# Moving the score output of the RWKV mixer from its own visit into the fourth level of the triangular inverse

## Chip, cores and metric

One core of a Trainium2 chip runs the whole kernel. The metric is the device time of one execution in microseconds (us), and its median over several executions.

## The reference

A trunk of two layers works on 256 tokens of width 2048. Layer 0 projects the tokens and mixes them in two ways: 8 heads of stick-breaking attention (head width 128) and 16 heads of an RWKV-7 recurrence (head width 64). Layer 1 is a gated delta rule. Behind each mixer follow an output projection, a layer norm, and a squared-ReLU MLP with a second layer norm. Only layer 0's mixer is touched here:

```python
z = jnp.einsum('bhqd,bhsd->bhqs', q_blk, kf) * (d ** -0.5)
log_keep = jnp.where(mask, jax.nn.log_sigmoid(-z), 0.0)
log_a = z + lax.cumsum(log_keep, axis=3, reverse=True)
a = jnp.exp(jnp.where(mask, log_a, -jnp.inf))
return jnp.einsum('bhqs,bhsd->bhqd', a, vf)
...
h = jnp.concatenate([o_sb, o_rw], axis=-1).astype(x.dtype) @ ev_w_out[e]
```

The last einsum of the attention, `a` by `vf`, is the "score output" of this document. Its result is needed only by the output projection `ev_w_out`.

## The kernel before

**Projections.** All large products split their f32 weights into a high part `wh` and a low part `wl` (both f32r) and add three products. Weights come in panels of 8 units from HBM into `raw`; for each unit ScalarE writes the high part (L888), VectorE subtracts it to give the low part (L1358), and TensorE then runs the matmuls of the unit (L422). A unit may start on TensorE only when VectorE has signalled its low part (`lo_ready`). Both engines make the split of unit u + 2 while TensorE works on unit u.

**The mixer inside the projections.** Layer 0 is cut into 8 groups of heads. While TensorE projects group i (16 units, 32 half units of 9 matmuls), it also runs the mixer `mix0` of group m = i - 1: one attention head and two RWKV heads. So there are 8 mixer bodies, m = 0 to 7. The first six are a hardware loop, the seventh stands behind it, and m = 7 runs inside the output projection, whose matmuls are wider. On every engine `mix0` is a generator, cut by `yield` into 28 visits, numbered 0 to 27 here. The tuple `HOPS0` says how many half units TensorE runs behind each visit:

```python
HOPS0 = (3, 3, 2, 2, 2) + 16 * (1,) + (0, 1, 0, 1, 0, 1, 1)
```

So unit 4 lies behind visit 3, unit 5 behind visit 4, half of unit 6 behind visit 5. ScalarE and VectorE run their own pieces of a visit and behind them the splits that belong to it: the split of unit 5 is behind visit 2, of unit 6 behind visit 3, of unit 7 behind visit 4. The order on each engine is fixed by this program text; engines meet only at semaphores.

**The visits that matter.** Visit 1: TensorE makes the scores (up to L508), VectorE takes them at L1511. Visit 2: VectorE's operand chain, up to `loga` (L1536) and `operands` (L1540), fed by ScalarE's exponentials. Visit 3: ScalarE's exponential L981 gives the attention weights `sba` and signals `attn`. Visit 4: TensorE waits for `attn` and runs L522 (two query blocks by the values `vtk` of block 0) and L523 (the second block), both f32, into PSUM bank `mb[3]`; they are called the pair. ScalarE copies the result to `hTh` (L984, `sb_hi`), and VectorE subtracts for `hTl` (L1544, `sb_lo`). Visit 5: TensorE waits for `operands` and `sb_lo` and makes the chunk matrices (L535, L540), the latter into `mb[3]`. Visit 6: transposes of the tokens; those of k and b go into bank `mb[1]` and stay there until ScalarE has copied them to `BK` (L1001, L1003, L1005, in levels 2 to 4). Visits 7 to 17 are the inverse of a triangular matrix, in levels: visit 6 + 2 lv has L582 (`dX`), visit 7 + 2 lv the transposes of X (L558) and the next L566 (`AX`). So level 4 is visits 14 and 15 on TensorE. VectorE answers with L1566 (`Yn`) and L1573 (`X_ready`), ScalarE with the transposed copy L1008. Between them VectorE runs pieces of the next group's token shift (`next(pieces, None)`). Visit 18 uses the inverse (L593), and writes banks 0 and 1. Visits 19 to 25 are the four chunks of the recurrence (L623 to L640), visits 26 and 27 the norm of the output (L645, L646, L649).

Of the kernel before, what the change touches and what calls it, by code (L numbers as in the profile page):

```python
# [16 lines left out]
ALU = mybir.AluOpType  # L17
ACT = mybir.ActivationFunctionType

P = 128  # L20
D = 2048
T = 256
# [142 lines left out]
def trunk(nc, stop, x, w384, w512, wba, consts, c0, c1, prm0, lora, conv, rows1, normw, ln, out):  # L165
    ctx = ExitStack()
    with ctx:
        def sb(name, shape, dt=F32):
            return ctx.enter_context(nc.sbuf_tensor(name, shape, dt))
# [3 lines left out]
        def S(name):  # L173
            if name not in sems:
                sems[name] = ctx.enter_context(nc.semaphore(name))
            return sems[name]
# [7 lines left out]
        hTh = sb("hTh", [P, KT, T], F32R)  # L184
        hTl = sb("hTl", [P, KT, T], F32R)
# [5 lines left out]
        mb = [mpf[:, b * WIDE:(b + 1) * WIDE] for b in range(4)]  # L191
# [7 lines left out]
        def half(i):  # L199
            return slice(HC * i, HC * i + HC)  # L200
# [5 lines left out]
        def r2(ap, **kw):  # L206
            return ap.rearrange("p (a b) -> p a b", **kw)
# [34 lines left out]
        BK, UV = (r2(lay(4 * P), a=4) for _ in range(2))  # L242
# [11 lines left out]
        vtk = r2(lay(T), a=TT)  # L254
        sba, sbb, sbc = (lay(384) for _ in range(3))
# [121 lines left out]
        def _(pe):  # L377
            mm = nc.tensor.matmul

            def to_tiles():  # L380

                pe.sem_inc(S("tiles"), 1)
# [109 lines left out]
            def mix0(m):  # L492
                m1 = m + 1
# [9 lines left out]
                   skip_group_check=True).then_inc(S("lora_used"), 1)  # L503
# [5 lines left out]
                   skip_group_check=True).then_inc(S("scores"), 1)  # L509
# [8 lines left out]
                mm(mb[2][:, 0:384], tri, sbb, start=True, stop=False, skip_group_check=True)  # L518
                mm(mb[2][:, P:T], ones, sbb[:, T:384], start=False, stop=True, skip_group_check=True).then_inc(S("lcum"), 1)
                yield  # L520
                pe.wait_ge(S("attn"), m1)
                mm(mb[3][:, 0:T], vtk[:, 0, :], sba[:, 0:T], start=True, stop=False, skip_group_check=True)  # L522
                mm(mb[3][:, P:T], vtk[:, 1, :], sba[:, T:384], start=False, stop=True,  # L523
                   skip_group_check=True).then_inc(S("sb_o"), 1)
                yield
                pe.wait_ge(S("operands"), m1)
                pe.wait_ge(S("sb_lo"), m1)
                to_tiles()
                turned = lambda n: slice((n + 3) % 4 * HC, (n + 3) % 4 * HC + HC)
                for t in range(TT):  # L530
                    for w in range(2):
                        for h, hf in QUADS:
# [3 lines left out]
                                      start=t + w == 0, stop=True, skip_group_check=True)  # L536
# [19 lines left out]
                def transpose_x():  # L556
                    for h in range(2):
                        last = nc.tensor.transpose(mb[0][:, h * P:(h + 1) * P],  # L558
                                                   X0[:, 2 * h:2 * h + 2, :].rearrange("p t c -> p (t c)"), ident)
                    last.then_inc(S("Xnew"), 1)  # L560

                def a_times_x(lv):
                    for h in range(2):
                        for e, t in QUADS:
                            Xp = X0[half(e), 2 * h + t, :].rearrange("p (b w s) -> p b w s", w=2, s=1 << lv)
                            last = mm(mb[2 + e][half(t), h * T:h * T + 32], GM[half(e), 2 * t + 1 - e, h, 0, :], Xp[:, :, 0, :],  # L566
                                      start=h == 0, stop=True, skip_group_check=True)
                    last.then_inc(S("AX"), 1)
# [7 lines left out]
                for lv in range(1, 6):  # L576
                    pe.wait_ge(S("Yn"), 5 * m + lv)
                    pe.wait_ge(S("XT_ready"), 6 * m + lv)
                    to_tiles()
                    for h in range(2):  # L580
                        for t, e in QUADS:
                            last = mm(mb[2 + t][half(e), h * T:h * T + 32], XT0[half(t), h, e, :], Yn0[half(t), 2 * e + h, :],  # L582
                                      start=h == 0, stop=True, skip_group_check=True)
                    last.then_inc(S("dX"), 1)
                    yield
                    pe.wait_ge(S("X_ready"), 6 * m + lv + 1)
                    transpose_x()
                    if lv < 5:
                        a_times_x(lv + 1)
                    else:  # L590
                        for h in range(2):
                            for hf, t in QUADS:
                                last = mm(mb[2 + hf][half(t), h * T:h * T + HC], GM[half(hf), 2 * t + hf, h, 0, :],  # L593
                                          UV[half(hf), 2 * t + hf, half(h)], start=h == 0, stop=True, skip_group_check=True)
                        last.then_inc(S("AV"), 1)
                    yield
# [1 line left out]

                pe.wait_ge(S("XT_ready"), 6 * m1)
                pe.wait_ge(S("AVs"), m1)  # L600
                pe.wait_ge(S("tok_ready"), 2 * m1)
                to_tiles()
                for h in range(2):
                    for t, hf in QUADS:
                        last = mm(mb[2 + t][half(1 - hf), h * T:h * T + HC], XT0[half(t), h, 1 - hf, :],
                                  AVs[half(t), (2 * hf + h) * HC:(2 * hf + h + 1) * HC], start=h == 0, stop=True,
                                  skip_group_check=True)
                last.then_inc(S("XAV"), 1)
                for hf in range(2):
                    for t, h in QUADS:  # L610
                        last = mm(mb[t][half(h), half(hf)], tokw[half(t), hf, half(h)], XT0[half(t), h, 1 - hf, :],
                                  start=hf == 0, stop=True, skip_group_check=True)
# [3 lines left out]
                for n in range(4):  # L616
                    t, hf = divmod(n, 2)
                    st_in, y_ = (Sb, Sa)[n % 2], mb[2][:, n * P:(n + 1) * P]
                    if n:
                        pe.wait_ge(S("state0"), 3 * m + n)  # L620
                        if n < 3:

                            last = mm(mb[0][:, 0:P], KR[:, hf, 0, :, :].rearrange("p t c -> p (t c)"), st_in, start=True, stop=True,  # L623
                                      skip_group_check=True)
                        else:
                            last = mm(mb[0][half(1 - hf), 0:P], KR[:, hf, 0, t, :], st_in, start=True, stop=True,
                                      skip_group_check=True)
# [6 lines left out]
                    if n < 3:  # L634
                        mm(mb[3][:, 0:P], BK[:, n, :], UV[:, n, :], start=True, stop=True,
                           skip_group_check=True).then_inc(S("dS"), 1)
                    if n:
# [3 lines left out]
                       skip_group_check=True).then_inc(S("y_psum"), 1)  # L641
# [16 lines left out]
            with pe.Fori(1, GROUPS - 1) as i:  # L658
                drive(group0(i), 2 * UNITS, 0, mix0(i - 1), HOPS0)
            drive(group0(GROUPS - 1), 2 * UNITS, 0, mix0(GROUPS - 2), HOPS0)  # L660

            pe.wait_ge(S("mix0_out"), GROUPS - 2)
# [216 lines left out]
        def _(act):  # L879
            go = nc.scalar.activation  # L880
            st = Steps(act, S("act_steps"))
# [64 lines left out]
            def mix0(m):  # L946
                m1 = m + 1
# [32 lines left out]
                act.wait_ge(S("loga"), m1)  # L980
                go(sba, sba, ACT.Exp).then_inc(S("attn"), 1)  # L981
                yield
                act.wait_ge(S("sb_o"), m1)
                nc.scalar.copy(hTh[:, bass.ds(m * 2, 1), :], mb[3][:, 0:T].unsqueeze(1)).then_inc(S("sb_hi"), 1)  # L984
                yield
                yield

# [9 lines left out]
                nc.scalar.copy(XTf0, mb[0][:, 0:T]).then_inc(S("XT_ready"), 1)  # L997
                yield
                for lv in range(1, 6):
                    if lv == 2:  # L1000
                        st(nc.scalar.copy(BK[half(0), :, :], r2(mb[1][half(0), :], a=4)))  # L1001
                    elif lv == 3:
                        st(nc.scalar.copy(BK[half(1), 1:4, :], r2(mb[1][half(1), 0:3 * P], a=3)))  # L1003
                    elif lv == 4:
                        nc.scalar.copy(BK[half(1), 0, :], mb[1][half(1), 3 * P:4 * P]).then_inc(S("tok_ready"), 1)  # L1005
                    yield
                    act.wait_ge(S("Xnew"), 6 * m + lv + 1)
                    nc.scalar.copy(XTf0, mb[0][:, 0:T]).then_inc(S("XT_ready"), 1)  # L1008
                    if lv == 5:
                        act.wait_ge(S("AV"), m1)  # L1010
                        nc.scalar.copy(r2(AVs, a=4), r2(mp[1][:, :], a=4)[:, :, 0:HC]).then_inc(S("AVs"), 1)
                    yield
# [311 lines left out]
            def solo():  # L1324
# [3 lines left out]
                for _ in range(7):  # L1328
# [6 lines left out]
                       True, begun=True)  # L1335
# [8 lines left out]
        def _(dve):  # L1344
            tt, ts, stt = nc.vector.tensor_tensor, nc.vector.tensor_scalar, nc.vector.scalar_tensor_tensor
            st = Steps(dve, S("dve_steps"))

            def f(ap):
                return ap.bitcast(F32)

            def rep(ap, n):

                return ap.unsqueeze(1).to_broadcast([P, n, ap.shape[-1]])
# [151 lines left out]
            def mix0(m, ahead=True):  # L1505
                m1 = m + 1
                par = lambda j: prm[:, bass.ds(m, 1), j]
                pieces = shift(m1) if ahead else iter(())
# [24 lines left out]
                for w, a, b_ in ((1, rkv[:, 0, :], pinc), (0, kkt, pexc)):  # L1533
# [6 lines left out]
                tt(btr[:, 3 * HC:T], bt[:, 0:HC], pinv[:, 0:HC], ALU.mult).then_inc(S("operands"), 1)  # L1540
                yield
                yield
                dve.wait_ge(S("sb_hi"), m1)
                tt(hTl[:, bass.ds(m * 2, 1), :], mb[3][:, 0:T].unsqueeze(1), f(hTh[:, bass.ds(m * 2, 1), :]),  # L1544
                   ALU.subtract).then_inc(S("sb_lo"), 1)
                yield
                dve.wait_ge(S("gram"), m1)
                for h in range(2):
# [14 lines left out]
                for lv in range(1, 6):  # L1563
                    s_ = 1 << lv
                    dve.wait_ge(S("AX"), 5 * m + lv)
                    tt(Yn0, r2(mp[1][:, :], a=4)[:, :, 0:32], rep(cc[:, C_LV + 32 * (lv - 1):C_LV + 32 * lv], 4),  # L1566
                       ALU.mult).then_inc(S("Yn"), 1)
                    if lv > 2:
                        next(pieces, None)
                    yield  # L1570
                    dve.wait_ge(S("dX"), 5 * m + lv)
                    left = X0.rearrange("p (h t) (b w s) -> p h t b w s", h=2, w=2, s=s_)[:, :, :, :, 0, :]
                    tt(left, left, mp[1][:, :].rearrange("p (t h c) -> p h t c", t=TT, h=2)[:, :, :, 0:32].rearrange("p h t (b s) -> p h t b s", s=s_),  # L1573
                       ALU.add).then_inc(S("X_ready"), 1)
                    if lv > 2:
                        next(pieces, None)
                    yield
                next(pieces, None)
                yield
                dve.wait_ge(S("XAV"), m1)  # L1580
# [500 lines left out]
```

## Time and profile before

| | |
|---|---|
| median of 3 runs | 3047.07 us (3045.55 to 3051.02) |
| the profiled execution's own time | 3048.84 us |
| its span, first to last instruction | 3047.10 us |
| TensorE busy | 2957.6 us, 97% |
| VectorE busy | 1797.7 us, 59% |
| ScalarE busy | 1453.1 us, 48% |
| mean granted TensorE clock | 0.992 |

The times of three runs differ by up to 5.5 us, 0.2%. A busy share says how full an engine is, not who holds up whom; for that the table of waits, the timeline of one body and the chain that ended last are read, in the rows below. Windows and start times are in us from the span's start; the body shown is m = 2, near 191 to 256 us, unless another is named.

### The profile page before, as it was taken

How to read it: one execution, taken by the hardware profiler on the slowest of the kernel's cores; microseconds unless marked ns; L12 is line 12 of the kernel's file. 1: busy time of each engine (PE TensorE's matmuls, PEld its weight loads, DVE VectorE, ACT ScalarE, POOL GpSimd, SP SyncE). 2: the span in 40 equal slices, each digit the busy share in tenths (PEclk: the TensorE clock that was granted, in tenths of full speed). 3: DMA queues.
4: the chain of work that ended last, by engine and by line, in shares of the span. 5: the costliest groups of instructions: out<-in, count | busy, mean ns of one | idle time of the engine just before them, and what ended most of it. 6: DMA issues, size and time to landing. Idle time of an engine off the chain costs nothing.

```text
span 3047.1 us, 55921 instructions
## 1 busy us (share of the span) xinstructions
PE 2957.6 (97%) x22084; PEld 2603.3 (85%) x22084; DVE 1797.7 (59%) x2375; ACT 1453.1 (48%) x2241; POOL 13.1 (0%) x28
## 2 busy tenths in 40 slices
PE   7999999999999999999999999999999999999997
PEld 7888887788888888889999997999977888888886
DVE  4555565565554555564667665566667545555555
ACT  4544454344443444435566664456653434444342
POOL 0000000000000000000000000000000000000000
PEclk9999999999999999999999999999999999999999
DMA  6333334455555555543343433544335555555553
GB/s 214 109 116 111 103 112 144 175 191 189 192 188 191 189 193 191 190 162 136 121 139 132 139 134 136 178 142 137 127 125 219 189 193 187 193 187 191 189 187 111
DMA packets 156999, 491.86 MB, mean 161 GB/s; under 512 B 15584, under 2 KB 50528, under 8 KB 155776
## 3 DMA queue, kind: packets, MB, share of 16 engines
q1 hardware_dynamic: 154032, 476.18, 46.0%
q0 software_dynamic: 2224, 11.69, 1.0%
q8 instruction: 160, 2.62, 0.3%
q10 hardware_dynamic: 544, 1.05, 0.1%
q14 instruction: 39, 0.32, 0.0%
HBM read 486.76 MB, written 2.10 MB: 160 GB/s over the span
## 4 chain that ended last, share of the span: by engine, by line
PE 91%; DVE 5%; ACT 2%; issue 1%; DMA 0%; ACTq 0%; SPq 0%; DVEq 0%
PE pp L422 45%; PE mp L422 11%; PE pp L406 8%; PE mp L406 8%; PE pp L408 4%; PE mp L408 4%; PE mp L821 1%; PE mp L785 1%; PE mp L769 1%; PE mp L761 1%; DVE wl L1358 1%; ACT wh L888 1%; PE mp L827 1%; PE mp L582 0%; PE mp L566 0%
## 5 line engine op out<-in xcount | busy, mean ns | idle before, releaser
L1358 DVE TENSOR_TENSOR wl<-raw,wh 128x1024 fp32r<-128x1024 f32 (+1 forms) x936 | 1101.3, 1184 | 843.0 <-ACT wh L888 839.8
L888 ACT CAST wh<-raw 128x1024 fp32r<-128x1024 f32 (+1 forms) x936 | 943.9, 1018 | 856.3 <-PE pp L422 283.4
L422 PE MATMUL pp<-aT,wh 128*128 128x256 f32 x4704 | 898.1, 291 | 11.4 <-DVE wl L1358 6.7
L422 PEld LDWEIGHTS pp<-aT,wh 128*128 128x128 f32 x4704 | 733.4, 192 | 27.7 <-issue 7.4
L422 PE MATMUL pp<-aT,wl 128*128 128x256 f32 x2352 | 665.7, 283 | 0.0
L422 PEld LDWEIGHTS pp<-aT,wl 128*128 128x128 f32 x2352 | 450.3, 191 | 0.0
L406 PE MATMUL pp<-aT,wh 128*128 128x512 f32 x1024 | 364.8, 400 | 0.6 <-issue 0.4
L422 PE MATMUL pp<-wh,hTh 128*128 128x512 f32 x896 | 358.5, 400 | 4.0 <-DVE wl L1358 2.6
L406 PE MATMUL mp<-aT,wh 128*128 128x512 f32 x1024 | 360.0, 396 | 0.0
L422 PE MATMUL pp<-wh,hTl 128*128 128x512 f32 x896 | 349.6, 390 | 0.0
L422 PE MATMUL pp<-wl,hTh 128*128 128x512 f32 x896 | 349.1, 390 | 0.0
L408 PE MATMUL pp<-aT,wl 128*128 128x256 f32 x1024 | 288.3, 282 | 0.0
L408 PE MATMUL mp<-aT,wl 128*128 128x256 f32 x1024 | 286.5, 280 | 0.0
L406 PEld LDWEIGHTS pp<-aT,wh 128*128 128x128 f32 x1024 | 194.3, 190 | 48.6 <-issue 2.0
L406 PEld LDWEIGHTS mp<-aT,wh 128*128 128x128 f32 x1024 | 192.2, 188 | 46.5
L422 PEld LDWEIGHTS pp<-wh,hTh 128*128 128x128 f32 x896 | 168.2, 188 | 42.1 <-DVE wl L1358 2.9
L422 PE MATMUL mp<-wh,hTh 128*128 128x512 f32 x512 | 199.2, 389 | 0.0
L422 PE MATMUL mp<-wl,hTh 128*128 128x512 f32 x512 | 199.2, 389 | 0.0
L422 PE MATMUL mp<-wh,hTl 128*128 128x512 f32 x512 | 199.2, 389 | 0.0
L422 PEld LDWEIGHTS pp<-wh,hTl 128*128 128x128 f32 x896 | 168.2, 188 | 35.9
L422 PEld LDWEIGHTS pp<-wl,hTh 128*128 128x128 f32 x896 | 168.4, 188 | 32.9 <-issue 0.5
L408 PEld LDWEIGHTS pp<-aT,wl 128*128 128x128 f32 x1024 | 195.1, 190 | 0.1
(301 smaller groups left out, 2671.9 us busy)
## 6 DMA issues: line engine op xcount, KB each, us to landing
raw<-in_w_dram SPq DMA_DIRECT2D x800, 512.0 KB, 3.3
raw<-in_w_dram SPq DMA_DIRECT2D x136, 384.0 KB, 3.5
ws<-in_ln_dram POOLq DMA_DIRECT2D x8, 1024.0 KB, 7.6
out_dram<-xres SPq DMA_DIRECT2D x8, 256.0 KB, 2.0
ws<-in_lora_dram POOLq DMA_DIRECT2D x8, 192.0 KB, 3.5
xres<-in_x_dram ACTq DMA_DIRECT2D x2, 512.0 KB, 6.2
xres<-in_x_dram SPq DMA_DIRECT2D x2, 512.0 KB, 7.1
ws<-in_c_dram POOLq DMA_DIRECT2D x1, 576.0 KB, 6.9
```

The costliest lines, as they stand in the source:

```text
L406: mm(o, wh[:, slot, kk, c], aT[:, k, :, :].rearrange("p a b -> p (a b)"), start=first is not None and kk == 0, stop=False, skip_group_chec ...
L408: last = mm(o[:, 0:T], wl[:, slot, kk, c], ah[:, k, :], start=False, stop=end and kk == 1, skip_group_check=True)
L422: last = mm(o, lhs, rhs, start=opens and m == 0, stop=end and kk == 1 and m == 2, skip_group_check=True)
L761: last = nc.tensor.transpose(mb[2][:, h * P:(h + 1) * P], Xc[:, 2 * h:2 * h + 2, :].rearrange("p c t -> p (c t)"), ident)
L769: last = mm(mb[hf][half(c), h * P:h * P + 32], At[half(hf), c, h, half(hf)], Xp[:, :, 0, :], start=h == 0, stop=True, skip_group_check=True)
L785: last = mm(mb[2 + c][half(hf), h * P:h * P + 32], XTc[half(c), h, hf, :], Yn1[half(c), 4 * hf + h, :], start=h == 0, stop=True, skip_grou ...
L821: last = mm(bank[:, h * P:(h + 1) * P], lhs[:, h, :], rhs[:, h, :], start=h == 0, stop=True, skip_group_check=True)
L827: last = mm(bank[:, j * T:(j + 1) * T], lhs[:, j, :], rhs[:, 2 * j:2 * j + 2, :], start=j == 0, stop=True, skip_group_check=True)
L888: nc.scalar.copy(wh[:, q % RING, :, 0:width], raw[:, q, :, 0:width]).then_inc(S("hi_ready"), 1)
L1358: tt(wl[:, q % RING, :, 0:width], raw[:, q, :, 0:width], f(wh[:, q % RING, :, 0:width]), ALU.subtract).then_inc(S("lo_ready"), 1)
```

## The change

The pair leaves visit 4 and goes into level 4 of the inverse, visit 14, behind L582. It writes bank `mb[1]` instead of `mb[3]`, so the k and b copies to `BK` move one level up, and the pair waits for `tok_ready` as well as for `attn`. ScalarE's copy to `hTh` moves to visit 15, behind the transposed copy; VectorE's subtraction for `hTl` moves to visit 15 too, behind `Yn` of level 5, where it takes the place of one piece of the token shift, which is made up for in visit 17. TensorE's wait for `sb_lo` moves from visit 5 to visit 18. Visit 4 stays, with its two half units and no mixer work on TensorE, ScalarE or VectorE.

```diff
@@ TensorE, visit 4 and 5
                 yield
-                pe.wait_ge(S("attn"), m1)
-                mm(mb[3][:, 0:T], vtk[:, 0, :], sba[:, 0:T], start=True, stop=False, skip_group_check=True)
-                mm(mb[3][:, P:T], vtk[:, 1, :], sba[:, T:384], start=False, stop=True,
-                   skip_group_check=True).then_inc(S("sb_o"), 1)
                 yield
                 pe.wait_ge(S("operands"), m1)
-                pe.wait_ge(S("sb_lo"), m1)
                 to_tiles()
@@ TensorE, level lv, behind L582
                     last.then_inc(S("dX"), 1)
+                    if lv == 4:
+                        pe.wait_ge(S("attn"), m1)
+                        pe.wait_ge(S("tok_ready"), 2 * m1)
+                        mm(mb[1][:, 0:T], vtk[:, 0, :], sba[:, 0:T], start=True, stop=False, skip_group_check=True)
+                        mm(mb[1][:, P:T], vtk[:, 1, :], sba[:, T:384], start=False, stop=True,
+                           skip_group_check=True).then_inc(S("sb_o"), 1)
                     yield
@@ TensorE, visit 18
                 pe.wait_ge(S("AVs"), m1)
-                pe.wait_ge(S("tok_ready"), 2 * m1)
+                pe.wait_ge(S("sb_lo"), m1)
@@ ScalarE, visit 4
                 yield
-                act.wait_ge(S("sb_o"), m1)
-                nc.scalar.copy(hTh[:, bass.ds(m * 2, 1), :], mb[3][:, 0:T].unsqueeze(1)).then_inc(S("sb_hi"), 1)
                 yield
@@ ScalarE, levels
                 for lv in range(1, 6):
-                    if lv == 2:
+                    if lv == 1:
                         st(nc.scalar.copy(BK[half(0), :, :], r2(mb[1][half(0), :], a=4)))
+                    elif lv == 2:
+                        st(nc.scalar.copy(BK[half(1), 1:4, :], r2(mb[1][half(1), 0:3 * P], a=3)))
                     elif lv == 3:
-                        st(nc.scalar.copy(BK[half(1), 1:4, :], r2(mb[1][half(1), 0:3 * P], a=3)))
-                    elif lv == 4:
                         nc.scalar.copy(BK[half(1), 0, :], mb[1][half(1), 3 * P:4 * P]).then_inc(S("tok_ready"), 1)
                     yield
                     act.wait_ge(S("Xnew"), 6 * m + lv + 1)
                     nc.scalar.copy(XTf0, mb[0][:, 0:T]).then_inc(S("XT_ready"), 1)
-                    if lv == 5:
+                    if lv == 4:
+                        act.wait_ge(S("sb_o"), m1)
+                        nc.scalar.copy(hTh[:, bass.ds(m * 2, 1), :], mb[1][:, 0:T].unsqueeze(1)).then_inc(S("sb_hi"), 1)
+                    elif lv == 5:
@@ VectorE, visit 4
                 yield
-                dve.wait_ge(S("sb_hi"), m1)
-                tt(hTl[:, bass.ds(m * 2, 1), :], mb[3][:, 0:T].unsqueeze(1), f(hTh[:, bass.ds(m * 2, 1), :]),
-                   ALU.subtract).then_inc(S("sb_lo"), 1)
                 yield
@@ VectorE, levels, behind Yn
-                    if lv > 2:
+                    if lv == 5:
+                        dve.wait_ge(S("sb_hi"), m1)
+                        tt(hTl[:, bass.ds(m * 2, 1), :], mb[1][:, 0:T].unsqueeze(1), f(hTh[:, bass.ds(m * 2, 1), :]),
+                           ALU.subtract).then_inc(S("sb_lo"), 1)
+                    elif lv > 2:
                         next(pieces, None)
                     yield
@@ VectorE, visit 17
                     yield
+                next(pieces, None)
                 next(pieces, None)
                 yield
```

## Rows read from the trace of the kernel before

**Rows 1.** The page: shares of the chain that ended last.

```profile
PE 91%; DVE 5%; ACT 2%; issue 1%; DMA 0%; ACTq 0%; SPq 0%; DVEq 0%
```

**Rows 2.** TensorE's waits, 59 to 506 us: waiting line, releaser, total us, times, longest.

```profile
PE mp L522 <- ACT ws L981: 8.2, 7, 1.2
PE mp L645 <- ACT ws L1027: 6.0, 7, 0.9
...
PE pp L422 <- DVE wl L1358: 2.2, 8, 0.5
```

**Rows 3.** TensorE's timeline, visit 4: start, us, instruction, [idle before <- releaser].

```profile
208.71 0.28 PE L422 MATMUL pp<-aT,wl 128*128 128x256 f32 x1
210.15 0.70 PE L522 MATMUL mp<-ws 128*128 128x256 f32 x2 [1.17 <-ACT ws L981]
210.69 0.39 PE L523 MATMUL mp<-ws 128*128 128x128 f32 x2
211.33 0.51 PE L422 MATMUL pp<-aT,wh 128*128 128x256 f32 x2 [0.25 <-DVE wl L1358]
```

**Rows 4.** VectorE's timeline at the same time (x2: two splits in a row).

```profile
210.19 0.22 DVE L1540 TENSOR_TENSOR ws<-ws 128x64 f32<-128x64 f32 x1
210.32 1.82 DVE L1358 TENSOR_TENSOR wl<-raw,wh 128x768 fp32r<-128x768 f32 x2
```

**Rows 5.** The chain that ended last, in order of time: start, us, what.

```profile
200.20 0.57 DVE ws L1511
...
210.41 0.88 DVE wl L1358
211.33 2.42 PE pp L422 x18
...
252.47 4.30 PE pp L422 x36
...
259.72 0.57 DVE ws L1511
```

**Rows 6.** TensorE's timeline in the last body, m = 7, around the pair.

```profile
517.50 0.47 PE L422 MATMUL pp<-wh,hTh 128*128 128x512 f32 x1 [1.36 <-DVE wl L1358]
...
520.12 0.39 PE L422 MATMUL pp<-wh,hTl 128*128 128x512 f32 x1
520.35 0.59 PE L522 MATMUL mp<-ws 128*128 128x256 f32 x2
...
520.92 0.48 PE L422 MATMUL pp<-wh,hTh 128*128 128x512 f32 x1
521.24 0.39 PE L422 MATMUL pp<-wl,hTh 128*128 128x512 f32 x1
```

**Rows 7.** TensorE's timeline at visit 14 of m = 2.

```profile
230.55 0.43 PE L582 MATMUL mp<-ws 64*64 64x32 f32 x16
```

**Rows 8.** Timelines of ScalarE, VectorE and TensorE at visits 12 to 17.

```profile
226.67 0.48 ACT L1003 COPY ws<-mp 64x384 f32<-64x384 f32 x1
232.51 0.37 ACT L1008 COPY ws<-mp 128x256 f32<-128x256 f32 x1 [2.09 <-PE mp L558]
232.78 0.84 ACT L888 CAST wh<-raw 128x768 fp32r<-128x768 f32 x1
234.54 0.29 DVE L1573 TENSOR_TENSOR ws<-ws,mp 128x128 f32<-128x128 f32 x1
235.58 0.38 PE L558 MATMUL mp<-cc,ws 128*128 128x128 f32 x2
```

**Rows 9.** Two gaps of TensorE, and the stretches behind (window, length, busy, granted clock).

```profile
12.72 0.77 PE L422 MATMUL pp<-aT,wh 128*128 128x256 f32 x2 [2.99 <-DVE wl L1358]
12.70:18.00 5.30, 5.28 (x26) 5.30 (x27) 2.84 (x3) 1.67 (x2) 0.00 (x0) 1.00 1.05 389
1333.80 1.11 PE L472 MATMUL mp<-cc,xres 128*128 128x128 f32 x4 [4.71 <-DVE xres L1442]
1333.80:1342.00 8.20, 6.59 (x28) 5.40 (x29) 8.06 (x12) 3.86 (x6) 0.00 (x0) 0.51 0.00 0
```

## The prediction

> **What bounds the kernel now.** I read four views, in this order. First the page: TensorE holds 91% of the chain that ended last [rows 1]. So the question for any edit is whether it takes work or waiting off TensorE, or puts some onto it, at a place where nothing else is later. Second, the table of waits of TensorE over the stretch of the first seven RWKV bodies (m = 0 to 6) [rows 2]. The largest entry is the very wait that the change removes: L522, the score output, stands 8.2 us in 7 waits behind the exponential of L981, 1.17 us each. Read alone, that promises 8.2 us. Third, therefore, the timeline of TensorE around one of these waits, at m = 2 [rows 3]. TensorE ends unit 4 at 208.71 + 0.28 = 208.99, waits, starts the pair L522 and L523 at 210.15, and starts the projection's unit 5 at 211.33, with a second wait of 0.25 us just before it, released by VectorE's split L1358. Fourth, what VectorE does at that time [rows 4]: it comes out of the operand chain with L1540 at 210.19 and only then, at 210.32, starts the low halves of the weights of units 5 and 6. The chain that ended last goes just there [rows 5]: VectorE's L1540, L1358 until 210.41 + 0.88 = 211.29, then TensorE's L422 from 211.33. It does not pass through L981, L522 or L523. One body lasts 59.52 us, from VectorE's L1511 at 200.20 to the next one at 259.72 [rows 5]. The pair and the wait ahead of it lie in a gap that ends with the split of unit 5, whatever TensorE does in it. This is the reading on which the forecast rests: two waits in a row, of which the second, small one is the one that counts.
>
> **Is that gap the same in every body?** The seven waits on L522 sum to 8.2 us with the longest 1.2, and the waits of L422 on L1358 in the same stretch come right behind them [rows 2]. The largest other wait in the body, L645 on the copy L1027, is a round trip that starts from a matmul of TensorE itself. The eighth body (m = 7) differs: its wait for the split, 1.36 us, is before unit 5's counterpart at 517.50, and L522 follows at 520.35 with no wait, inside back-to-back matmuls [rows 6].
>
> **The change part by part.**
>
> 1. *Visit 4 loses the wait on attn and the two matmuls.* In m = 0 to 6 TensorE reaches unit 5 at 208.99 instead of 211.1, and waits there for VectorE's split, which ends at 211.29 because L1540 ends at 210.41, and L1540 and the split stand in VectorE's row with no idle time ahead of them, so that nothing out of visit 4 holds them [rows 4, 5]. Start of unit 5: 211.33 before, 211.33 after. Gain 0. The idle time becomes 211.33 - 208.99 = 2.34 us in one piece. In m = 7 the pair stands in a dense stream. The price of the pair in a dense stream is read there: L422 matmuls follow each other every 0.23 us, as from 520.12 to the start of the pair at 520.35. From 520.12 to 521.24 there lie two such steps (0.46) and the pair: 1.12 - 0.46 = 0.66 us [rows 6]. Gain there 0.66 us.
>
> 2. *Visit 14 gains the two matmuls.* In the stretch of visits 5 to 18 no wait of TensorE stands among the groups of [rows 2] nor in its timeline, and the place of insertion, right behind L582 at 230.55, is in the middle of it [rows 7]. So each body pays the price of the pair in a dense stream: 0.66 us, eight times 5.3 us. Bounds: not below 0; not above the 0.93 us from the start of L522 at 210.15 to the end of L523 at 211.08 [rows 3], that is if nothing of the pair overlaps its neighbours. I take 0.66, as it is the same pair measured in a dense stream. The step from quadrant matmuls to full ones comes at visit 14 anyway (L582 to L422), so none is added.
>
> 3. *The new waits at visit 14.* attn is given before the pair at 210.15 [rows 3], 20 us ahead of visit 14. The k and b copies move one level up; the last one, L1005 (64x128), goes where L1003 (64x384) ran before, from 226.67 to 227.15 [rows 8]; the pair would start at about 230.9. Nothing waits: cost 0, cover 3.7 us. Should that cover go, ScalarE's last copy would be late for TensorE by its own length, under 0.48. The bank is next written at visit 18.
>
> 4. *The copy to hTh on ScalarE and the subtraction to hTl on VectorE move to visit 15.* At visit 4 they were off the chain: gone, they give nothing, since unit 7's split is behind them, not unit 5's. At visit 15 ScalarE copies X transposed at 232.51, then the new copy, then its split L888, which started at 232.78 [rows 8]. A 128x256 copy takes 0.37 but the next one starts after 0.27, so the split comes 0.27 later, and VectorE's split behind it too. Behind that is L1573, the update of X, at 234.54 + 0.29 = 234.83, which then ends near 235.10; TensorE wants it at 235.58 for L558 [rows 8]. Slack 0.75, of which 0.27 are used. The transposed copy that TensorE needs at visit 16 is ahead of the new one in ScalarE's order. VectorE's subtraction of 128x256 takes the place of a token-shift piece of the same size, and that piece goes to visits 16 and 17, behind the update of X. Cost 0; if the cover were gone, see rival A. No DMA and no queue is touched.
>
> 5. *The wait on sb_lo goes from visit 5 to 18.* It was met in time: the table of waits has no entry for L535 [rows 2]. Gain 0, and 0 at visit 18, two visits after the subtraction.
>
> **Does the delay survive to the next body?** The chain answers: TensorE's 36 projection matmuls from 252.47, the group up to L508, and at 259.72 VectorE's L1511, from where ScalarE and VectorE go in turn to L1540 [rows 5]. All of it starts from TensorE, so unit 5 of the next body comes as much later as visit 14 was longer.
>
> **The sum.** Added 8 x 0.66 = 5.28, saved 1 x 0.66 (m = 7): +4.6 us. The profiled execution took 3048.84 for a span of 3047.10, 1.74 us around it that the change does not touch; it would become 3053.4. It lies 1.8 us above the median of the runs, 3047.07, so the forecast for the median is 3047.07 + 4.6 = **3051.7 us**, +0.15%. With the pair at its upper bound in the seven bodies and at visit 14 of the eighth: 8 x 0.93 - 0.66 = 6.8, 3053.9; at the lower bound -0.66, 3046.4.
>
> **A rule that speaks against a longer gap.** TensorE's granted clock was 0.51, so the lower level of 1.2 GHz, from 1333.80 on, after 4.71 us without work; it was 1.00 (2.4 GHz) in the stretch behind the 2.99 us ahead of 12.72 [rows 9]. The 2.34 us of the new gap is below both, so I keep the full clock. The Trainium skill says, in "TensorE: Matmul & The Clock Gate", section "What's actually happening", that the clock is gated to half rate when the engine has been idle, and that activity releases it. By that rule the lengthened gap is a risk that the old one, broken up by the pair, was not; the trace agrees for the long gaps and shows no fall at the shorter one. It stands below as a rival.
>
> **The rivals.**
>
> *A. The handoffs at visits 15 to 17 reach TensorE (slower).* The new copy must be done before VectorE can subtract, and both stand ahead of the splits. In series the copy and a subtraction of the same size are 2 x 0.37 = 0.74 against a slack of 0.75 at L558 [rows 8]; with a handoff or two of 0.1 to 0.2 and the split pushed as well, TensorE would lose up to 0.4 a body. It decides from 0.75 on. Time: 3051.7 + 8 x 0.4 = 3054.9. Against it: the subtraction only replaces a piece of the same size. Chance 0.15.
>
> *B. The clock falls in the new gap (slower).* The low stretch behind L472 lasted at least 8.20 us [rows 9]; at half rate it costs half of that, 4.1 us, seven times 28.7: 3080. Chance 0.02.
>
> *C. The pair costs nothing at visit 14, or its delay is taken up by the wait at L645 (no change).* That is 0.86 us a body [rows 2], more than 0.66. Against it: L1027 copies what TensorE wrote just before, so it moves with TensorE. Time 3047. Chance 0.14.
>
> *D. The gap was TensorE's own after all (faster).* If the split of unit 5 ended earlier once visit 4 is empty, the 1.17 us come back, and with a split done by 208.99 the whole gap, less the pair: 7 x (2.34 - 0.66) = 11.8, 3035; with only the waits on L981 gained, and the pair neutral, 3047.07 - 8.2 = 3038.9. The point from which it decides: the split must end 0.66 us earlier, by 210.6. For it speaks that the profile names L981 as the releaser; against it, that VectorE comes to the split from the operand chain without an idle moment [rows 4], and that chain reads nothing from visit 4. Chance 0.07.
>
> **How the numbers follow.** Forecast 0.62, A 0.15, B 0.02, C 0.14, D 0.07. About 0.2% (6.1 us) is what a measurement of this kernel can tell from no change; the three runs before spread over 5.5 us. The forecast's 4.6 us is under it, but its upper bound 6.8 is over it: 0.08 of its 0.62 falls on slower, the rest on same. Slower 0.08 + 0.15 + 0.02 = 0.25. Of D 0.05 lies beyond 0.2%. Faster 0.05, same 0.70. The range takes in C below with the spread of a median (3046.0) and A above (3055.5); B, D and A's far end are left out. The forecast's own range is 3050 to 3054.
>
> **What the profile after would show.** Right: the wait of L522 on L981 is gone and in its place each of seven bodies has one wait of L422 on L1358 of about 2.3 us; the period of a body is 59.52 + 0.66 = 60.2 us; L582 at level four is followed by the pair with no wait; L558 at visit 17 has none; the first matmul of unit 5 starts as long after L1511 as before (211.33 - 200.20 = 11.13 us [rows 5]). Wrong: the L422 wait is much below 2.3 us (D), a wait at L558 or L593 behind VectorE or ScalarE (A), a granted clock under 1.00 in the bodies (B), a period that stays at 59.5 (C).

## The result and the profile after

The changed kernel takes 3061.1 us in the median of 6 runs (3059.59 to 3062.28), against 3047.06 us before: ratio 1.0043, 95% interval 1.0033 to 1.0053, slower by 14.0 us. The forecast was 3051.7 with a range up to 3055.5. Its direction was right, a third of its size was found, and the rest came from the rival that had been given a chance of 0.02.

TensorE's waits in the changed kernel, 59 to 520 us (waiting line, releaser, total, times, longest):

```profile
PE pp L422 <- DVE wl L1360: 16.8, 8, 2.3
PE mp L646 <- ACT ws L1029: 6.0, 7, 0.9
```

The 8.2 us behind the exponential are gone, and the waits for the split have grown from 2.2 to 16.8 us [rows 2]. So far this is what the prediction said of visit 4. TensorE's timeline there, m = 2:

```profile
213.46 0.28 PE L422 MATMUL pp<-aT,wl 128*128 128x256 f32 x1
216.07 0.51 PE L422 MATMUL pp<-aT,wh 128*128 128x256 f32 x2 [2.33 <-DVE wl L1360]
216.41 0.29 PE L422 MATMUL pp<-aT,wl 128*128 128x256 f32 x1
216.54 0.57 PE L422 MATMUL pp<-aT,wh 128*128 128x256 f32 x2
216.91 0.42 PE L422 MATMUL pp<-aT,wl 128*128 128x256 f32 x1
217.12 0.63 PE L422 MATMUL pp<-aT,wh 128*128 128x256 f32 x2
217.55 0.41 PE L422 MATMUL pp<-aT,wl 128*128 128x256 f32 x1
...
219.47 0.41 PE L422 MATMUL pp<-aT,wl 128*128 128x256 f32 x1
219.81 0.41 PE L530 MATMUL mp<-ws 64*64 64x128 f32 x4
```

The gap is 2.33 us, as forecast. But half a microsecond behind it the same matmuls take 0.41 instead of 0.28 us, and follow each other at nearly twice the distance. From the start of unit 5 to the start of the chunk matrices in L530 it takes 219.81 - 216.07 = 3.74 us; in the kernel before it took 2.35 (211.33 to 213.68, where that line is L535). The windows show why (window, length, then busy time and count by engine; the granted clock is the third number from the end):

```profile
214.00:216.00 2.00, 0.00 (x0) 0.00 (x0) 1.97 (x6) 1.68 (x3) 0.00 (x0) 1.00 0.00 0
216.00:217.00 1.00, 0.93 (x6) 0.93 (x7) 1.00 (x3) 1.00 (x2) 0.00 (x0) 0.80 0.00 0
217.00:219.70 2.70, 2.70 (x14) 2.59 (x13) 0.76 (x1) 0.04 (x1) 0.00 (x0) 0.50 0.75 220
```

TensorE did nothing from 213.7 to 216.07, and from 216.6 to some 220 the granted clock was 0.50, the lower level of 1.2 GHz. A stretch at 0.50 lies at unit 5 in all seven bodies with the gap. It does not always begin at the same point: in m = 0 the clock was still 1.00 for 1.0 us behind the start of unit 5, and in m = 5 it was already at 0.50 0.2 us ahead of it, with TensorE still idle. The Trainium skill says, in "TensorE: Matmul & The Clock Gate", section "What's actually happening", that an idle engine is gated to half rate; here the trace agrees, behind idle stretches of 2.33 us.

VectorE's side of the same moment, and the chain:

```profile
214.93 0.22 DVE L1542 TENSOR_TENSOR ws<-ws 128x64 f32<-128x64 f32 x1
215.06 2.69 DVE L1360 TENSOR_TENSOR wl<-raw,wh 128x768 fp32r<-128x768 f32 x3
```

```profile
204.95 0.57 DVE ws L1513
...
215.15 0.88 DVE wl L1360
216.07 3.81 PE pp L422 x18
...
236.83 0.36 PE mp L577 x16
237.20 0.63 PE mp L583 x2
237.83 0.22 PE mp L584 x2
238.05 1.07 PE pp L422 x9
```

Beside [rows 4, 5]: the operand chain hands over to the split and the split to unit 5 exactly as before (216.07 - 204.95 = 11.12 us from L1513, against 11.13), the 18 matmuls of unit 5 last 3.81 instead of 2.42 us, and the pair, now L583 and L584, lies on the chain at visit 14. Visits 12 to 17, answering to [rows 8]:

```profile
232.88 0.26 ACT L1004 COPY ws<-mp 64x128 f32<-64x128 f32 x1
239.38 0.37 ACT L1007 COPY ws<-mp 128x256 f32<-128x256 f32 x1 [3.03 <-PE mp L553]
239.91 0.85 ACT L889 CAST wh<-raw 128x768 fp32r<-128x768 f32 x1
241.67 0.28 DVE L1576 TENSOR_TENSOR ws<-ws,mp 128x128 f32<-128x128 f32 x1
242.44 0.38 PE L553 MATMUL mp<-cc,ws 128*128 128x128 f32 x2
```

The update of X ends at 241.95 and TensorE uses it at 242.44 without a wait: 0.49 of slack is left, where 0.48 was forecast.

The bodies m = 0 to 5 last 61.58 to 61.70 us instead of 59.52, and from m = 6 to m = 7 it is 66.30 instead of 64.32. The wait for the split in m = 7 ends at 532.87 instead of 517.50, 15.4 us later. Behind the mixer the changed kernel's profiled execution is 2.3 us shorter (0.6 of it in the first MLP, 1.7 in the last part of the span), in code that the change does not touch; so the whole span is only 3060.2 - 3047.1 = 13.1 us longer.

### The profile page after: what moved, and what is told of

Read it like the earlier page. It is cut to its first block, busy times and chain, and to the rows that moved or that the text cites. A ratio compares the mean times of both kernels' runs of the same rounds, so it can differ in the third digit from the quotient of the medians.

```text
span 3060.2 us, 55929 instructions
## 1 busy us (share of the span) xinstructions
PE 2964.5 (97%) x22084; PEld 2612.9 (85%) x22084; DVE 1798.9 (59%) x2375; ACT 1452.0 (47%) x2241; POOL 13.1 (0%) x28
## 4 chain that ended last, share of the span: by engine, by line
PE 91%; DVE 5%; ACT 2%; issue 1%; DMA 0%; ACTq 0%; SPq 0%; DVEq 0%
PE pp L422 45%; PE mp L422 11%; PE pp L406 8%; PE mp L406 8%; PE pp L408 4%; PE mp L408 4%; PE mp L822 1%; PE mp L786 1%; PE mp L770 1%; PE mp L762 1%; DVE wl L1360 1%; ACT wh L889 1%; PE mp L828 1%; PE mp L577 0%; PE mp L561 0%
## 5 line engine op out<-in xcount | busy, mean ns | idle before, releaser
L422 PE MATMUL pp<-aT,wh 128*128 128x256 f32 x4704 | 907.2, 293 | 26.1 <-DVE wl L1360 21.4
L422 PEld LDWEIGHTS pp<-aT,wh 128*128 128x128 f32 x4704 | 741.1, 194 | 42.2 <-DVE wl L1360 20.1
L422 PE MATMUL pp<-aT,wl 128*128 128x256 f32 x2352 | 670.4, 285 | 0.0
L422 PEld LDWEIGHTS pp<-aT,wl 128*128 128x128 f32 x2352 | 454.9, 193 | 0.0
L422 PE MATMUL pp<-wh,hTh 128*128 128x512 f32 x896 | 358.4, 400 | 4.0 <-DVE wl L1360 2.6
L422 PE MATMUL pp<-wh,hTl 128*128 128x512 f32 x896 | 349.6, 390 | 0.0
L422 PE MATMUL pp<-wl,hTh 128*128 128x512 f32 x896 | 349.2, 390 | 0.0
L422 PEld LDWEIGHTS pp<-wh,hTh 128*128 128x128 f32 x896 | 168.2, 188 | 42.1 <-DVE wl L1360 2.9
L422 PE MATMUL mp<-wh,hTh 128*128 128x512 f32 x512 | 199.2, 389 | 0.0
L422 PE MATMUL mp<-wl,hTh 128*128 128x512 f32 x512 | 199.2, 389 | 0.0
L422 PE MATMUL mp<-wh,hTl 128*128 128x512 f32 x512 | 199.2, 389 | 0.0
L422 PEld LDWEIGHTS pp<-wh,hTl 128*128 128x128 f32 x896 | 168.2, 188 | 36.0
L422 PEld LDWEIGHTS pp<-wl,hTh 128*128 128x128 f32 x896 | 168.4, 188 | 32.9 <-issue 0.5
```

The costliest lines, as they stand in the source:

```text
L422: last = mm(o, lhs, rhs, start=opens and m == 0, stop=end and kk == 1 and m == 2, skip_group_check=True)
```

## The experiments

Theory 1: of the 2.15 us that a body got longer, 0.66 are the pair on the chain, and 1.5 the half clock behind the lengthened gap. Theory 2: they come from the pair's place at visit 14, and the clock is a bystander. The body time, from one L1511 to the next in m = 0 to 5, is taken from the trace of each kernel (an edit shifts line numbers: the same line is L1513 in the changed kernel, L1507 in no_pair). Bodies of one kind agree to 0.2 us within an execution, so this is the sharper measure; the runs of one kernel spread over 3 to 9 us. Low clock is counted in m = 0 to 6. A median in brackets is that of the kernel before in the same series of runs.

| kernel | gap before unit 5 | bodies at low clock | body, us | median, us (before) | ratio, 95% |
|---|---|---|---|---|---|
| before | 1.17 + 0.25 | 0 of 7 | 59.52 | 3047.06 | |
| changed | 2.33 | 7 of 7 | 61.58 to 61.70 | 3061.1 | 1.0043 (1.0033 to 1.0053) |
| no_pair | 2.34 | 6 of 7 | 60.87 to 61.04, one 59.51 | 3061.76 (3046.94) | 1.0043 (1.0030 to 1.0057) |
| fill_pair | 1.68 | 0 of 7 | 60.16 | 3054.51 (3046.94) | 1.0025 (1.0015 to 1.0035) |
| pair_twice | 1.17 + 0.25 | 0 of 7 | 60.17 | 3053.39 (3046.94) | 1.0020 (1.0011 to 1.0029) |
| fill_tiny | 1.15 + 0.77, a small matmul between | 6 of 7 | 61.65, one 60.17 | 3058.52, one run | |
| fill_small | 2.11 | 5 of 7 | 61.65, two 60.18 | 3059.58, one run | |
| after_early | 1.00 | 0 of 7 | 58.87 | 3043.78 (3048.05) | 0.9985 (0.9976 to 0.9994) |
| before_early | 1.17 | 0 of 7 | 58.99 | 3045.5 (3048.05) | 0.9994 (0.9985 to 1.0003) |

**no_pair: only the gap.**

```diff
@@ the kernel before, TensorE, visit 4
-                pe.wait_ge(S("attn"), m1)
-                mm(mb[3][:, 0:T], vtk[:, 0, :], sba[:, 0:T], start=True, stop=False, skip_group_check=True)
-                mm(mb[3][:, P:T], vtk[:, 1, :], sba[:, T:384], start=False, stop=True,
-                   skip_group_check=True).then_inc(S("sb_o"), 1)
@@ ScalarE, visit 4
-                act.wait_ge(S("sb_o"), m1)
+                act.wait_ge(S("scores"), m1)
```

> The kernel before with the pair (L522, L523) and its wait on attn left out of visit 4 and put nowhere; the copy to hTh takes what the scores left in the bank, so the score output is not computed. Theory 1 (the longer gap lowers the clock, and that costs 1.5 us in each of seven bodies; the pair itself costs 0.66 us where it is on the chain): TensorE idles 2.3 us before unit 5 in m = 0 to 6, granted clock 0.5 behind it, body 59.5 + 1.5 = 61.0 us, total +10.5 - 0.66 (m = 7) = +9.8 us, about 3057. Theory 2 (the 2.15 us a body of the changed kernel come from the pair's new place at visit 14, by a switch of tile mode or by the handoffs behind it, and the clock is a bystander): body 59.5 us, total -0.7 us, about 3046.

Work was taken away and the kernel got slower. Two bodies of one execution tell it best. Behind a gap of 2.34 us each, m = 2 and m = 5:

```profile
214.19 0.51 PE L422 MATMUL pp<-aT,wh 128*128 128x256 f32 x2 [2.34 <-DVE wl L1354]
...
215.12 0.63 PE L422 MATMUL pp<-aT,wh 128*128 128x256 f32 x2
215.55 0.41 PE L422 MATMUL pp<-aT,wl 128*128 128x256 f32 x1
...
397.24 0.50 PE L422 MATMUL pp<-aT,wh 128*128 128x256 f32 x2 [2.34 <-DVE wl L1354]
397.58 0.28 PE L422 MATMUL pp<-aT,wl 128*128 128x256 f32 x1
...
398.41 0.40 PE L422 MATMUL pp<-aT,wh 128*128 128x256 f32 x2
398.65 0.28 PE L422 MATMUL pp<-aT,wl 128*128 128x256 f32 x1
```

```profile
397.00:401.00 4.00, 3.76 (x67) 3.56 (x68) 2.49 (x5) 1.47 (x3) 0.00 (x0) 1.00 0.49 162
214.00:218.00 4.00, 3.81 (x22) 3.58 (x26) 2.21 (x4) 1.42 (x2) 0.00 (x0) 0.61 0.51 156
```

Where the clock fell the body lasts 61.0 us; in m = 5, where it did not, 59.51, the time of before to 0.01. So the gap without the clock costs nothing, and the clock costs 1.5 us. Theory 2 falls: with nothing at visit 14 the slow bodies are still there. In the mixer this makes 8.8 us (526.34 against 517.50). The median is 14.8 us up, 5 more than expected. In the profiled execution 8 us are in the first MLP (729.4 us from transpose to transpose, against 721.2). TensorE's waits there, 630 to 1340 us:

```profile
PE pp L408 <- issue: 3.0, 2, 1.6
PE pp L406 <- issue: 1.0, 2, 0.5
```

These four waits end with nothing that the profile shows; the kernel before has one, of 0.4 us. Behind the last two of them the granted clock was 0.50 once more, from 1167.2 to 1170.6. Together that is some 5 of the 8 us. What causes such waits in code that the edit doesn't touch, and whether the other runs had them, is open, so no more than the 8.8 us in the mixer is laid to the gap.

**pair_twice: only the pair at visit 14.**

```diff
@@ the kernel before, TensorE, behind L582
                     last.then_inc(S("dX"), 1)
+                    if lv == 4:
+                        pe.wait_ge(S("tok_ready"), 2 * m1)
+                        mm(mb[1][:, 0:T], vtk[:, 0, :], sba[:, 0:T], start=True, stop=False, skip_group_check=True)
+                        mm(mb[1][:, P:T], vtk[:, 1, :], sba[:, T:384], start=False, stop=True, skip_group_check=True)
```

> The kernel before with a second copy of the pair at visit 14, into the bank of the k and b tokens, with the wait on tok_ready; its result is not used. The gap at visit 4 is as before. Theory 1: the granted clock stays at 1.00 in the bodies, each of the 8 bodies pays the pair once more at 0.66 us: body 60.2 us, total +5.3 us, about 3052.3. Theory 2: the place at visit 14 costs 2.15 us: body 61.7 us, total +17 us, about 3064.

The body is 60.17 us, 0.65 longer, with the clock at full rate in all seven bodies. The price of 0.66 us for the pair in a dense stream, read in the body m = 7, holds at visit 14. The median is 6.5 us up, 5.3 expected, inside its interval (3.4 to 8.8).

**fill_pair: the changed kernel, gap filled in part.**

```diff
@@ the changed kernel, TensorE, visit 4
+                mm(mb[3][:, 0:T], vtk[:, 0, :], sbb[:, 0:T], start=True, stop=False, skip_group_check=True)
+                mm(mb[3][:, P:T], vtk[:, 1, :], sbb[:, T:384], start=False, stop=True, skip_group_check=True)
                 yield
```

> The changed kernel with a pair of idle matmuls of the same two shapes put at the start of visit 4, without a wait, into the bank that nobody reads from (values by the finished log-keep terms). Theory 1: the gap before unit 5 is cut to 2.33 - 0.64 = 1.7 us, the granted clock stays at 1.00, body 59.52 + 0.66 = 60.2 us; m = 7 pays the filler, 0.66: total +4.6 + 0.7 = +5.3 us over the kernel before, about 3052.3. If 1.7 us is still long enough for the clock to fall: about 3063. Theory 2: body stays 61.7 us, total +14.7 us, about 3061.8.

```profile
209.95 0.39 PE L522 MATMUL mp<-ws 128*128 128x128 f32 x2
212.02 0.51 PE L422 MATMUL pp<-aT,wh 128*128 128x256 f32 x2 [1.68 <-DVE wl L1362]
```

Useless work of 0.64 us in the gap makes each body 1.5 us shorter than in the changed kernel. It costs nothing there, and the clock stays. The median is 7.6 us up on the kernel before (4.6 to 10.7), where 5.3 was expected.

**fill_tiny and fill_small: how much is enough?**

```diff
@@ fill_tiny: the changed kernel, TensorE, visit 4
+                pe.wait_ge(S("attn"), m1)
+                mm(mb[3][:, 0:32], vtk[:, 0, :], sbb[:, 0:32], start=True, stop=True, skip_group_check=True)
@@ fill_small: the changed kernel, TensorE, visit 4
+                mm(mb[3][:, 0:P], vtk[:, 0, :], sbb[:, 0:P], start=True, stop=True, skip_group_check=True)
```

> The changed kernel with one small f32 matmul (128x32) in visit 4 behind the wait on attn, so that the gap is cut in two parts of about 1.4 and 1.0 us with some 0.05 us of work between them. Theory 1 leaves open whether such a short piece of work is enough. If it is: granted clock 1.00 in the bodies, body 60.2 us, about 3052. If it is not: 0.5 behind the gap as in the changed kernel, body 61.7 us, about 3061.

> The changed kernel with one f32 matmul of 128 columns at the start of visit 4, without a wait. The gap before unit 5 is then 2.33 - 0.21 = 2.1 us. A gap of 1.7 us left the clock at 1.00 in all seven bodies, one of 2.33 lowered it in seven of seven and in six of seven. If only the size of the gap decides, and 2.1 is under the limit: body 60.2 us in all, about 3052.5; if over it: 61.7 us in all, about 3062; if the limit also hangs on when the gap falls, some bodies of one kind and some of the other.

Neither is enough, and neither gives a clean answer: of 7 bodies, 1 and 2 kept the clock, at gaps that were equal to 0.02 us. So the size of the gap alone does not decide. Nor does its longest piece: in fill_tiny the pieces are 1.15 and 0.77 us (1.4 and 1.0 were expected), and the clock fell in six of seven bodies, while one piece of 1.68 in fill_pair left it up in all. A body is either 60.2 or 61.6 to 61.7 us, nothing between.

**after_early and before_early: shorten the gap where it is made.** The gap ends with VectorE's split of unit 5, which waits behind the operand chain only by program order. The new parameters `early` and `skip` in the two `def` lines are left out here.

```diff
@@ VectorE, mix0, visit 2 (after_early: here; before_early: behind the loga line)
+                if early:
+                    early()
                 dve.wait_ge(S("lcum"), m1)
                 tt(sba, sbc, mb[2][:, 0:384], ALU.subtract).then_inc(S("loga"), 1)
@@ VectorE, narrow
+                    if u == skip:
+                        return
@@ VectorE, loop over the groups, and likewise for m = 6
-                interleave(mix0(i - 1), HOPS0, 2 * UNITS, narrow(i * 2 + P_GROUPS0), (), nothing, True, True)
+                interleave(mix0(i - 1, early=lambda: split(i * 2 + P_GROUPS0, 5, NARROW)), HOPS0, 2 * UNITS,
+                           narrow(i * 2 + P_GROUPS0, skip=5), (), nothing, True, True)
```

> The changed kernel, with VectorE's split of unit 5 moved inside visit 2 of m = 0 to 6, ahead of the wait for lcum and L1538 (the attention's log terms), instead of behind L1542. Theory 1 (unit 5 is held by this split alone; the clock falls only behind the long gap): the split starts near the end of L1536 and ends 1.33 us earlier, the gap before unit 5 shrinks from 2.33 to 1.0 us, the clock stays at 1.00, and the log terms, now 0.9 us later, are needed only at visit 14: body 59.52 + 0.66 - 1.33 = 58.85 us, total 7 x (-0.67) = -4.7 us against the kernel before, about 3042.3. Rival (the gap is set by the whole operand chain, and operands become late for visit 5 instead): body about 60.2 us, about 3051.7, with a wait at L530.

> The kernel before, with VectorE's split of unit 5 moved inside visit 2 of m = 0 to 6, right behind L1536 (the log terms) and ahead of L1537 to L1540. Theory 1: the log terms and with them L981 and the pair keep their times (pair at 210.15 to about 210.8), the split is done at 210.45, and unit 5 starts behind the pair instead of at 211.33: 0.5 us a body, body 59.0 us, total -3.4 us, about 3043.6; the wait on L1358 is gone and that on L981 (1.17) stays. Rival (the 1.17 us wait on the exponential was never part of a gap that a split could shorten, as the operands then come late for visit 5): body 59.5 us, no change, about 3047.

after_early around unit 5, all engines:

```profile
208.06 0.95 DVE L1360 TENSOR_TENSOR wl<-raw,wh 128x768 fp32r<-128x768 f32 x1
208.93 0.55 DVE L1540 TENSOR_TENSOR ws<-ws,mp 128x384 f32<-128x384 f32 x1
209.07 0.51 PE L422 MATMUL pp<-aT,wh 128*128 128x256 f32 x2 [1.00 <-DVE wl L1360]
209.51 0.53 ACT L982 ACTIVATE ws<-ws 128x384 f32<-128x384 f32 x1 [1.77 <-DVE ws L1540]
```

Unit 5 starts as soon as its split is done, while the log terms (L1540 in this kernel) are not finished and the exponential L982 is still to come: with the pair at visit 14 nobody waits for them. Body 58.87 us, 58.85 expected; median 4.3 us under the kernel before, the interval (-7.3 to -1.8) clear of zero. This is the version that beats both the kernel before and the changed one. No wait at L530 appeared, so the rival did not occur. In before_early the body is 58.99 us, 59.0 expected, and unit 5 follows the pair with no wait of its own; the median is 2.6 us down, an interval that still touches zero.

## Why the prediction was wrong

**The reading of the gap was right.** The pair and its wait lay in a gap that ends with the split (unit 5 starts 11.12 us after the scores are taken, 11.13 before). Removing them gained nothing, as no_pair's m = 5 shows directly.

**The price of the moved pair was right:** 0.66 forecast, 0.65 in pair_twice.

**The covers were right:** no wait at L553, L594 or for tok_ready, and 0.49 us of slack at visit 17. Rivals A and C did not occur: the waits at L646 and L627 are the same as before and took up nothing. The body of after_early, 58.87 us against 58.85 added up from the pair's price and the earlier split, leaves no room for a cost of the handoffs either. Rival D as worded did not occur either, though its condition, a split done earlier, is what the two early versions bring about.

**The step that failed is "The 2.34 us of the new gap is below both, so I keep the full clock."** It rested on the stretch behind the 2.99 us gap at 12.72, where the column shows a clock of 1.00 [rows 9]. The same row has 26 matmuls in 5.30 us, 0.20 us each, where a dense stream at full clock steps by 0.12; and the row above it gives the first two 0.77 us. The matmuls there were at the lower rate. Further rows of the kernel before show it plainly:

```profile
7.80 1.94 PE L472 MATMUL mp<-cc,xres 128*128 128x128 f32 x8 [7.80 <-DMA xres<-in_x_dram]
12.72 0.77 PE L422 MATMUL pp<-aT,wh 128*128 128x256 f32 x2 [2.99 <-DVE wl L1358]
13.29 0.41 PE L422 MATMUL pp<-aT,wl 128*128 128x256 f32 x1
13.50 0.63 PE L422 MATMUL pp<-aT,wh 128*128 128x256 f32 x2
```

0.41 and 0.63 us are the durations of the low stretches after the change, to the digit. The clock records of this trace begin at 17.5 us, so the 1.00 in the column is a blank. The row doesn't even show a fall: the eight L472 ahead of the gap take 0.42 us each, as those at 1333.80 do at a granted clock of 0.51, where the shortest L472 of the trace takes 0.27. The clock was at the lower level before this gap as well as behind it. What was left of the trace of before were low stretches at gaps of 4.7 and 5.2 us, and full rate behind this gap of 1.76 us, the longest between matmuls that left it so:

```profile
1427.38 0.50 PE L422 MATMUL pp<-aT,wh 128*128 128x256 f32 x2 [1.76 <-DVE wl L1358]
1427.72 0.28 PE L422 MATMUL pp<-aT,wl 128*128 128x256 f32 x1
```

A gap of 2.34 lies between them and was open; rival B deserved far more than 0.02.

**B's price was mis-sized too.** It took the low stretch behind L472 (at least 8.2 us, 4.1 lost). Behind this gap it is shorter, from 216.6 to some 220 in m = 2, and costs 1.5 us a body. With that, 7 x (0.66 + 1.5) = 15.1 us, against the 15.4 measured to the split wait of m = 7 in the two profiles, of which 0.4 are there before the first body.

## What to carry to other kernels

Two waits in a row before one instruction are one gap: ask what ends it, and move that. Work that lies in such a gap is free and may even be worth its time, since it shortens the stretch in which TensorE is idle; before taking it out, ask what the idle time becomes. And check a granted clock against the duration of a matmul whose price at full rate is known, above all in the first microseconds.

## What the runs showed of the hardware

In the bodies, gaps of 1.0, 1.2, 1.4 (in two parts) and 1.7 us left the clock at full rate in all 35 bodies of five kernels; gaps of 2.1 to 2.34 us lowered it in 18 of 21, and 1.15 + 0.77 us with one small matmul between in 6 of 7. The four that were spared had gaps of the same length. Each fall cost 1.5 us. An edit that only removes work from idle time makes the mixer 8.8 us slower, 0.3% of the kernel.

1.7 us is not a safe length elsewhere. Behind the mixer every one of the nine kernels has a gap of 1.75 or 1.76 us before an L422, in code that no edit touches. In five profiled executions the clock stayed at 1.00 behind it; in four (pair_twice, fill_tiny, fill_small, after_early) it fell. pair_twice:

```profile
1432.55 0.65 PE L422 MATMUL pp<-aT,wh 128*128 128x256 f32 x2 [1.75 <-DVE wl L1362]
1432.99 0.42 PE L422 MATMUL pp<-aT,wl 128*128 128x256 f32 x1
1432.80:1436.00 3.20, 3.20 (x17) 3.20 (x17) 3.20 (x7) 2.81 (x3) 0.00 (x0) 0.50 0.48 166
```

What separates the spared bodies from the others, and these four executions from the five, stays open.
